# Order of two ACT operations in the steps of two attentions, on one Trainium2 core

## What is computed

```
p_cmp = masked_softmax(q @ k_cmp, cmp_mask);  o_cmp = p_cmp @ v_cmp
p_sel = masked_softmax(q @ k_sel, causal);    o_sel = p_sel @ v_sel
p_win = masked_softmax(q @ k_win, causal);    o_win = p_win @ v_win
o = g[0] * o_cmp + g[1] * o_sel + g[2] * o_win

logits = where(band, q @ k * hd ** -0.5, -inf);  m = max(max(logits), sink)
probs = exp(logits - m) / (sum(exp(logits - m)) + exp(sink - m));  out = probs @ v
```

## Time and profile before

| | |
|---|---|
| median of 3 runs | 1844.27 us (1842.77 to 1844.48) |
| the profiled execution | 1842.77 us, span 1840.9 us |
| PE busy | 1796.1 us, 98% |
| DVE busy | 934.2 us, 51% |
| ACT busy | 773.5 us, 42% |
| POOL busy | 889.1 us, 48% |
| granted PE clock | 0.996 of full speed |
| first attention, core of it | 151.7 to 306.7 us |
| second attention, core of it | 1230 to 1287.4 us |

### The profile page before, as it was taken

How to read it: one execution, slowest core, us unless ns; L and a number is a source line. 1 busy time by engine, 2 the same in 40 slices (tenths; PEclk the granted TensorE clock), 3 DMA queues, 4 the chain that set the end, 5 groups by cost and what they waited for, 6 DMA issues and landing times.

```text
span 1840.9 us, 24433 instructions
## 1 busy us (share of the span) xinstructions
PE 1796.1 (98%) x8930; PEld 1491.9 (81%) x8930; DVE 934.2 (51%) x1308; ACT 773.5 (42%) x1396; POOL 889.1 (48%) x675
## 2 busy tenths in 40 slices
PE   7999999999999999999999999998999999999997
PEld 6887878888888888888867888887888888888886
DVE  6258997525568823885753221348565320022437
ACT  5457887444433222224434332369224432233223
POOL 4346866474444444444432554449554344444442
PEclk9999999999999999999999999999999999999999
DMA  5420000252222233224222122210222223222321
GB/s 186 146 92 24 24 1 24 94 181 69 69 92 91 91 129 122 91 91 160 92 69 69 46 84 100 92 46 25 103 92 91 92 93 112 91 91 91 114 91 46
DMA packets 24270, 161.52 MB, mean 88 GB/s; under 512 B 2944, under 2 KB 3456, under 8 KB 5376
## 3 DMA queue, kind: packets, MB, share of 16 engines
q1 hardware_dynamic: 23184, 158.35, 24.9%
q10 hardware_dynamic: 1008, 2.12, 0.4%
HBM read 158.36 MB, written 2.10 MB: 87 GB/s over the span
## 4 chain that ended last, share of the span: by engine, by line
PE 91%; DVE 4%; ACT 2%; POOL 2%; issue 1%; DMA 0%; DVEq 0%; SPq 0%; ACTq 0%
PE psum L591 88%; PE psum L831 2%; DVE h_lo L2142 0%; DVE spare_r L2131 0%; DVE tmp L1969 0%; DMA xt<-in_x 0%; POOL w_lo L2669 0%; DVE negmax L2149 0%; POOL q_st L2745 0%; PE psum L1163 0%; POOL tmp L2745 0%; DVE big L2607 0%; ACT q_st L1527 0%; POOL big_r L2760 0%; DVE tmp L1967 0%
## 5 line engine op out<-in xcount | busy, mean ns | idle before, releaser
L2646 POOL TENSOR_TENSOR w_lo<-ring,w_hi_r 128x1024 fp32r<-128x1024 f32 (+2 forms) x264 | 632.7, 2418 | 735.6 <-ACT w_hi_r L1279 729.5
L591 PE MATMUL psum<-h_hi,w_hi_r 128*128 128x512 f32 (+1 forms) x1208 | 471.3, 390 | 11.5 <-DVE h_lo L2024 10.1
L591 PE MATMUL psum<-big_r,w_hi_r 128*128 128x512 f32 (+1 forms) x1568 | 467.4, 381 | 3.9 <-DVE xt L1924 1.9
L591 PE MATMUL psum<-h_lo,w_hi_r 128*128 128x512 f32 (+1 forms) x1208 | 469.1, 388 | 0.0
L591 PE MATMUL psum<-h_hi,w_lo 128*128 128x512 f32 (+1 forms) x1208 | 469.0, 388 | 0.0
L1279 ACT CAST w_hi_r<-ring 128x1024 fp32r<-128x1024 f32 x286 | 284.2, 1042 | 358.2 <-PE psum L591 350.8
L591 PEld LDWEIGHTS psum<-big_r,w_hi_r 128*128 128x128 f32 x1568 | 289.7, 188 | 61.6 <-issue 4.4
L591 PE MATMUL psum<-big_r,w_lo 128*128 128x512 f32 (+1 forms) x784 | 298.3, 380 | 0.0
L591 PEld LDWEIGHTS psum<-h_hi,w_hi_r 128*128 128x128 f32 x1208 | 227.2, 188 | 59.5 <-issue 12.8
L591 PEld LDWEIGHTS psum<-h_hi,w_lo 128*128 128x128 f32 x1208 | 227.2, 188 | 47.1
L591 PEld LDWEIGHTS psum<-h_lo,w_hi_r 128*128 128x128 f32 x1208 | 227.3, 188 | 46.0
(11 more groups left out here) (354 smaller groups left out, 2489.4 us busy)
## 6 DMA issues: line engine op xcount, KB each, us to landing
ring<-in_panels SPq DMA_DIRECT2D x146, 1024.0 KB, 4.8
xt<-in_x SPq DMA_DIRECT2D x4, 512.0 KB, 9.0
out<-big SPq DMA_DIRECT2D x8, 256.0 KB, 2.2
ring<-in_panels SPq DMA_DIRECT2D x2, 512.0 KB, 7.1
big<-in_mem ACTq DMA_DIRECT2D x1, 1024.0 KB, 4.7
q_st<-in_ple ACTq DMA_DIRECT2D x1, 512.0 KB, 3.4
spare<-in_w_gate ACTq DMA_DIRECT2D x1, 192.0 KB, 7.1
spare<-in_w_k ACTq DMA_DIRECT2D x1, 128.0 KB, 9.5
```

Of the source, the lines that this page charges most:

```text
L591: return nc.tensor.matmul(o, l, r, start=start, stop=stop, **kw)
L2646: g.tensor_tensor(w_lo[:, p], ring[:, p], plain(w_hi[:, p]), ALU.subtract) \
```

## The change

In both attentions the ACT queue's loop over the steps calls the rounding first and the copy second. Nothing else is changed; all waits and increments stay with their operations.

```diff
                     nsa_exp(parts[k + LEAD - 1])
                     if k + LEAD - 1 == NW - 1:
                         act.dma_start(mem_raw, a["mem"]).then_inc(mem_in, 16)
+                if 0 <= k < NW:
+                    nsa_hi(parts[k])
                 if k - 1 in unit_done:
                     nsa_correction(unit_done[k - 1])
-                if 0 <= k < NW:
-                    nsa_hi(parts[k])
                 if k in OUT_HI:
                     hi(PAIR0["nsa_out"], 1, parts=(OUT_HI.index(k),))
@@
                     sw_exp(sw_parts[k + LEAD - 1])
+                if 0 <= k < SW_NW:
+                    sw_hi(sw_parts[k])
                 if k - 1 in sw_done:
                     sw_correction(sw_done[k - 1])
-                if 0 <= k < SW_NW:
-                    sw_hi(sw_parts[k])
                 if k in MERGE_HI:
                     hi(PAIR0["merge_b"], 1, parts=(MERGE_HI.index(k),))
```

## The result

| | before | after |
|---|---|---|
| median | 1844.33 us (6 runs, 1842.77 to 1845.08) | 1858.41 us (6 runs, 1854.25 to 1858.95) |
| ratio | | 1.0074, 95% interval 1.0064 to 1.0084 |
| profiled execution, its span | 1842.77 us, 1840.9 us | 1858.62 us, 1856.6 us |
| PE busy | 1796.1 us | 1804.0 us |
| ACT, DVE, POOL busy | 773.5, 934.2, 889.1 us | 773.4, 933.0, 887.0 us |

The kernel became 14.1 us slower. The forecast was 8.1 us (1852.3), and the range ended at 1855.5: the sign was right, the size was not, and the measured time lies above even the worst rival. ACT, DVE and POOL do the same work in the same busy time. PE shows 8 us more, which is the first hint at a cost that the prediction didn't have.

What follows compares the result with a forecast made beforehand. The prediction took DVE's order (low half, maximum, reciprocal, join) as a real bound beside PE in the attentions. First attention 4.70 us plus second 3.36 us gave 8.06 us on the 1844.27 us median: 1852.3 us, range 1847.0 to 1855.5.

Steps and rivals of the forecast that it cites:

- The delay of one site: Each swapped step: join 0.49 us later, less DVE's own lag; 0.48 at the first site, 0.39 as lower bound.
- The nine sites that pass to PE whole: First attention, copies from 173.6 to 302.3 us: delays of 0.17 to 0.48 us reach PE undiminished, together 3.53 us.
- 185.1 us: First attention, copy at this time: 0.17 us of delay against 0.75 us of room, so nothing.
- The four lagging sites: First attention, copies at 208.9, 216.0, 286.2, 293.3 us, DVE 0.9 us behind: nothing, at most 0.3 us each.
- Step 103: First attention's last site, copy at 304.4 us: join 1.17 us later, all passed to PE's last product.
- Second attention, first site: Copy at 1240.9 us: 0.49 us, with PE's transpose at 1242.98 already waiting for that low half.
- POOL's stretch: Second attention, seven sites from 1244.5 to 1264.8 us: covered by POOL, so nothing, with 0.6 us as bound.
- The end of the second attention: Sites from 1270.8 us on: 2.87 us in all, 1.06 as base and 1.81 from the last two sites.
- slower still: Rival: delays also return through ACT in the first attention, lagging sites and POOL's stretch pay; 10.9 us, 1855.2 us, chance 0.11.
- the ring: Second attention from 1270.8 us: copy, join, low half, maximum, exponential feed delay back to ACT; base of 1.06 us.
- Partly covered: Rival: PE's work hides five first-attention sites (2.07 us) and 1.06 us in the second; 4.9 us, 1849.2 us, chance 0.22.
- not slower: Rival: joins' delays hidden everywhere but at the two attentions' ends; 2.5 us, 1846.8 us, chance 0.10.

Runs made afterwards that it cites:

- the run of these four sites: Copy put behind the rounding only at steps 40, 44, 92 and 96 of the first attention, against the kernel before: 1843.12 us in one execution.
- the ends and the others: Two kernels against before: swapped only at step 103 and the second attention's steps 29 and 31, 1849.00 us; swapped at all steps but these, 1850.64 us.
- the first swap alone: Copy and rounding swapped in the first attention only, against the kernel before: 1851.27 us, ratio 1.0039.
- both orders changed: The full change, plus DVE doing each join one place later, behind the next low half: 1844.36 us, ratio 1.0 against the kernel before.
- DVE's order changed alone: Kernel before, ACT's order kept, with DVE doing each join one place later, behind the next low half: 1854.77 us, ratio 1.0055.
- the second swap alone: Copy and rounding swapped in the second attention only, against the kernel before: 1850.04 us, ratio 1.0034.

## Why the prediction was wrong in size

- **The delay of one site: right, in part by luck.** 0.46 us at the first site, forecast 0.48. The copy starts 0.02 us after the rounding's end (173.60 + 0.58, then 174.20), so nothing of it slips under. That makes 0.60 from the rounding's start to the copy's, and not the 0.49 that I had read from the rounding to the exponential; but the rounding starts 0.12 us before the old copy's place (173.60 - 0.15, against 173.57), and the two differences cancel. The Trainium skill, Perfetto Trace Analysis, section on optimizing Scalar/DVE operations, which has the second half of a profiled latency overlap with the next instruction, would have given 0.39 here; for this pair the trace speaks against it.
- **The nine sites that pass to PE whole: right, a little short.** 3.53 forecast, 3.98 measured: 0.46, 0.59, 0.41, 0.46, 0.24, 0.45, 0.37, 0.60, 0.40. The sites of 195.7 and 273.0 us have 0.12 us more each than forecast, because the rounding there, that of the compressed branch with 31 rows, takes exactly the old copy's place, and I gave every site the 0.49 us of the first. The site of 195.7, of before and of after:

```profile
195.71 0.58 ACT L1548 COPY acc<-psum 64x512 f32<-64x512 f32 x1
...
196.32 0.58 ACT L1538 CAST tmp_r<-psum 31x512 fp32r<-31x512 f32 x1
```

```profile
196.29 0.58 ACT L1538 CAST tmp_r<-psum 31x512 fp32r<-31x512 f32 x1
...
196.90 0.58 ACT L1548 COPY acc<-psum 64x512 f32<-64x512 f32 x1
197.50 0.58 ACT L1527 ACTIVATE q_st<-psum,negmax 128x384 f32<-128x384 f32 x1
197.51 0.68 DVE L2170 TENSOR_TENSOR o_acc<-psum,acc 64x512 f32<-64x512 f32 x1 [0.73 <-ACT acc L1548]
```

The base here is 0.59, so the copy comes 0.60 us later, the full 0.61 between two starts. The remaining 0.2 us are at 263.2, of which I had taken 0.32 off for DVE's lag. The rows of before give less:

```profile
263.16 0.58 ACT L1548 COPY sqt<-psum 64x512 f32<-64x512 f32 x1
...
263.98 0.69 DVE L2170 TENSOR_TENSOR o_acc<-psum,sqt 64x512 f32<-64x512 f32 x1
```

The join's start less the copy's end less 0.03 is 0.21. In the kernel after the copy is at 266.72 us, with a base of 2.98 that is 0.58 later, and 0.58 - 0.21 = 0.37 is what was measured. I had misread the lag by 0.1 us, and the rest is again the 0.49.
- **185.1 us: right.** No shift remains (-0.02).
- **The four lagging sites: wrong, by 0.62 us.** Two errors. The size: by my own figures the copy would come 1.2 us later against a lag of 0.9, which leaves 0.3, and I set it to nothing. At step 40 the copy came 1.32 us later (210.05, base -0.17, against 208.90) and the join 0.43 us. And the room: I read it against PE's transpose alone, though the same list showed 24 waits of ACT for DVE's maxima. The delay left by that door, as the run of these four sites shows.
- **Step 103: right.** 1.20 against 1.17.
- **Second attention, first site: right.** 0.45 against 0.49 (POOL's scaling at 1243.61 starts at 1252.74, base 8.68).
- **POOL's stretch: wrong, by 0.75 us.** PE at 1266.24 is only 0.39 late (now 1275.31), so the cover held to its end. The next transpose, 1268.08, is 1.20 late (now 1277.96) behind a wait of 0.69 for DVE. I checked each reciprocal against its scaling, and not the last site's low half against the transpose behind the cover's end. The named bound of 0.6 us was about the right size, from the wrong place.
- **The end of the second attention: right.** 4.10 - 1.20 = 2.90 against 2.87. The reading of what is tight there left out POOL, which is the busiest of all with 20.35 of 21.2 us; the sum did not suffer from it.
- **The clock: missing.** The sum took PE's rate as fixed, although two of its own terms said that PE would stand still for 0.70 + 1.17 = 1.87 us and, at the end of the second attention, 0.94 and more. In the kernels read here the granted clock was 1.00 behind last products that had waited 0.71 us or less in the first attention and 0.94 or less in the second. Each wait of 1.78 us or more was followed by a fall, mostly at once; only in the kernel after the one of 1.84 (start at 1294.85) was followed by more than 5 us at 1.00, and the fall came behind the next long wait. At 0.50 PE's 128x512 products start 0.43 us apart instead of 0.23. That cost 2.8 and 1.6 us in the profiled execution, together 4.4, and 4.1 us between the medians with and without filling matmuls. That all other stretches would stay equal, as the prediction said, did not come true here. The trace of before had the sign already, where PE starts again at 937.09 us after a wait of 3.07:

```profile
938.70:942.00 3.30, 3.30 (x9) 2.53 (x8) 1.76 (x4) 3.25 (x4) 0.00 (x0) 0.50 0.00 0
```

Sum: 8.06 + 0.45 + 0.62 + 0.75 and small change = 9.85, plus the clock. Of the rivals, "slower still" had two of the three missing mechanisms (the ring closes in the first attention, the sites in POOL's stretch pay) and a fair size for them, 10.9 us with no clock; I gave it 0.11. "Partly covered" is refuted by the ends and the others adding up in the first attention, and by the five sites it names, which shift PE by 2.47 us together; "not slower" by the first site. A range that ended at the rivals' sum could not hold a cost that none of them had.

What stays open is when the clock falls behind a wait and for how long. The same 1.90 us has 0.59 behind it in the kernel after and 0.79 with the first swap alone (both 312 to 320 us), and a wait of 1.42 us left 1.00 with both orders changed, while three of 1.26 to 1.44 us close together went with 0.93 (1285 to 1310 us) with DVE's order changed alone. And the fall at 1258.9 us with the first swap alone had no wait above 0.91 us ahead of it. Open is also why the clock between 150 and 170 us and in the last 5 us is low in some executions and not in others.

## What to carry to other kernels

When two engines exchange several results in a step, what counts is not which is made first, but whether the reader takes them in the order in which they are made: change both lists or neither. Read a delay's room against everyone who reads what the delayed engine does next, its own readers' maxima and reciprocals included, and at the end of a cover against the first instruction that isn't covered. And where a sum makes TensorE wait longer in the midst of dense work, add a term for its clock, or give it something to do meanwhile.

## What the chip showed that I had not expected

A single wait of PE of 1.8 to 1.9 us between stretches of dense matmuls can be followed by a stretch at 1.2 GHz instead of 2.4. In the kernel after the granted clock behind the wait of 1.90 us is 0.50 over 4 us and 0.68 over the next 4, which costs 2.8 us, more than the wait itself; behind the wait of 1.78 it is 0.66 over 5 us, which costs 1.6. In the kernel with the second swap alone it is 0.70 over the 5.6 us behind a wait of 1.85. The Trainium skill, TensorE: Matmul & The Clock Gate, section on a second failure mode of the clock gate, reports that frequent short idles between groups of matmuls can be enough for it; the fall at 1258.9 us with the first swap alone, behind 0.43 and 0.91 us, agrees with that, while the others here followed single waits of 1.78 to 1.91 us. Matmuls that nobody needs (7 in the first attention, 18 in the second), put into such waits, brought the kernel after from 1858.41 to 1854.29 us.

The copy slips under nothing: in before 30 of the 32 copies follow another ACT operation at once, and each starts 0.02 us after its end. Of the 25 operations that follow a copy at once, 24 keep 0.02 to 0.03 us as well. Other pairs overlap: the exponential of 174.67 in the earlier trace rows starts 0.10 us before the rounding's end at 174.77. The number of rows alone doesn't decide it, since behind the cast of 31 rows at 196.32 in before the exponential starts 0.10 us early as well:

```profile
196.80 0.57 ACT L1527 ACTIVATE q_st<-psum,negmax 128x384 f32<-128x384 f32 x1
```

What does decide it no run here shows. A distance read between two operations should not be carried to another pair.
